# The weights' low parts are written by VectorE alone, in place and in longer pieces

## The reference

```python
for i in range(DEPTH):                      # DEPTH = 2
    u = rms_norm(h, norm_mix[i])
    mix = diff_attention(...) if i % 2 == 0 else moba_attention(...)
    h = h + mix
    u = rms_norm(h, norm_ffn[i])
    ffn = swiglu(u, gate, up, down) if i % 2 == 0 else moe_swiglu(u, router, gate, up, down)
    h = h + ffn
return rms_norm(h, final_norm)
```

## Time and profile before

| | us |
|---|---|
| median of 3 runs | 1608.91 |
| lowest and highest | 1608.26 to 1609.38 |
| span of the profiled execution | 1611.9 |
| TensorE busy in it | 1530.4 (95%) |
| VectorE busy | 1308.2 (81%) |
| ScalarE busy | 1145.0 (71%) |
| GpSimd busy | 619.0 (38%) |

### The profile page before, as it was taken

How to read it: one execution, slowest core, us unless ns; L and a number is a source line. 1 busy time by engine, 2 the same in 40 slices (tenths; PEclk the granted TensorE clock), 3 DMA queues, 4 the chain that set the end, 5 groups by cost and what they waited for, 6 DMA issues and landing times.

```text
span 1611.9 us, 25603 instructions
## 1 busy us (share of the span) xinstructions
PE 1530.4 (95%) x7688; PEld 1240.8 (77%) x7688; DVE 1308.2 (81%) x1820; ACT 1145.0 (71%) x2077; POOL 619.0 (38%) x458
## 2 busy tenths in 40 slices
PE   8998999999996999999999999999999999999997
PEld 7867999988875777777777777777777777777775
DVE  4555444443336999999999999999999999999998
ACT  5555544455543888788788878878888887887886
POOL 2112222221112454444444444445444444454543
PEclk9989999999997999999999999999999999999999
DMA  9723543554311899899899989989989998998970
GB/s 360 261 89 105 199 168 131 207 185 159 130 67 52 295 338 343 290 348 334 305 332 335 334 303 348 328 299 339 339 311 321 338 332 306 345 336 298 331 256 39
DMA packets 178356, 424.48 MB, mean 263 GB/s; under 512 B 4577, under 2 KB 6786, under 8 KB 178306
## 3 DMA queue, kind: packets, MB, share of 16 engines
q1 hardware_dynamic: 178018, 422.77, 73.4%
q10 hardware_dynamic: 288, 1.05, 0.2%
HBM read 422.76 MB, written 1.05 MB: 263 GB/s over the span
## 4 chain that ended last, share of the span: by engine, by line
PE 68%; DVE 13%; issue 11%; ACT 7%; DVEq 1%; POOL 1%; DMA 0%; ACTq 0%; POOLq 0%; SPq 0%
PE psA L1069 9%; PE psA L1070 9%; PE psA L1071 9%; DVE wlo L961 8%; PE psY L1069 6%; PE psY L1071 5%; PE psY L1070 5%; ACT whi L589 5%; PE psB L1069 5%; PE psB L1071 5%; PE psB L1070 5%; PE psY L1165 2%; PE psB L1301 2%; PE psY L1199 1%; PE psY L1088 1%
## 5 line engine op out<-in xcount | busy, mean ns | idle before, releaser
L961 DVE TENSOR_TENSOR wlo<-ring,whi 128x512 fp32r<-128x512 f32 x1012 | 940.2, 984 | 22.6 <-ACT whi L589 17.0
L589 ACT CAST whi<-ring 128x512 fp32r<-128x512 f32 x1349 | 810.2, 623 | 160.5 <-PE psY L1071 54.4
L714 POOL TENSOR_TENSOR wlo<-ring,whi 128x512 fp32r<-128x512 f32 x336 | 510.0, 1518 | 576.4 <-ACT whi L589 572.5
L735 DVE TENSOR_TENSOR wlo<-ring,whi 128x512 fp32r<-128x512 f32 x195 | 140.5, 734 | 194.3 <-ACT whi L434 194.0
L434 ACT CAST whi<-ring 128x512 fp32r<-128x512 f32 x260 | 157.5, 621 | 116.0 <-PE psB L1071 49.8
L672 POOL TENSOR_TENSOR wlo<-ring,whi 128x512 fp32r<-128x512 f32 x65 | 84.4, 1299 | 373.3 <-ACT whi L434 373.3
L1069 PE MATMUL psY<-whi,hhi 128*128 128x512 f32 x496 | 204.5, 412 | 20.4 <-DVE wlo L961 19.6
L1069 PE MATMUL psA<-whi,ihi 128*128 128x512 f32 x448 | 184.6, 412 | 15.7 <-DVE ilo L967 11.4
L1071 PE MATMUL psY<-whi,hlo 128*128 128x512 f32 x496 | 195.8, 395 | 0.0
L1070 PE MATMUL psY<-wlo,hhi 128*128 128x512 f32 x496 | 195.7, 395 | 0.0
L1069 PE MATMUL psB<-whi,ihi 128*128 128x512 f32 x448 | 180.9, 404 | 0.0
(11 more groups left out here) (229 smaller groups left out, 2293.2 us busy)
## 6 DMA issues: line engine op xcount, KB each, us to landing
ring<-in_moe_w_gate SPq DMA_DIRECT2D x56, 2048.0 KB, 7.7
ring<-in_moe_w_up SPq DMA_DIRECT2D x56, 2048.0 KB, 7.7
ring<-in_moe_w_down SPq DMA_DIRECT2D x56, 2048.0 KB, 7.8
ring<-in_moba_w_qkv SPq DMA_DIRECT2D x6, 2048.0 KB, 8.0
ring<-in_diff_w_qkv SPq DMA_DIRECT2D x5, 2048.0 KB, 16.6
ring<-in_ffn_w_gate SPq DMA_DIRECT2D x5, 2048.0 KB, 8.1
ring<-in_ffn_w_up SPq DMA_DIRECT2D x5, 2048.0 KB, 8.9
ring<-in_ffn_w_down SPq DMA_DIRECT2D x5, 2048.0 KB, 7.4
```

The costliest lines, as they stand in the source:

```text
L589: nc.scalar.copy(whi[:, (NG + m) % HL, :], ring[:, r, g * GROUP:(g + 1) * GROUP]).then_inc(hi_done, 1)
L714: nc.gpsimd.tensor_tensor(wlo[:, (NG + m) % HL, :], ring[:, (NS + j) % RING, g * GROUP:(g + 1) * GROUP], f(whi[:, (NG + m) % HL, :]), ALU. ...
L735: nc.vector.tensor_tensor(wlo[:, m % HL, :], ring_group(s, g), f(whi[:, m % HL, :]), ALU.subtract).then_inc(lo_dve, 1)
L961: nc.vector.tensor_tensor(wlo[:, (NG + m) % HL, :], ring[:, (NS + m // GS) % RING, g * GROUP:(g + 1) * GROUP], f(whi[:, (NG + m) % HL, :]) ...
```

## The change

- GpSimd makes no low parts any more. Its loop over items is gone. VectorE makes all of them.
- The low part has no tile of its own. `wlo` is now seven tiles that lie at the addresses of the seven raw ones: the low part is written over the raw weights.
- So a place of the ring is free only when TensorE has used its last group. SyncE waits for `group_used` instead of `lo_dve` and `lo_pool`.
- The space saved goes to `whi`, which is 12 groups deep instead of 6. `AHEAD` is 8 instead of 5.
- VectorE works in pieces: one group for the first 8 groups of the program, 4 groups (128x2048) in the dense feed-forward and in all items, and 2 groups (128x1024) elsewhere. ScalarE works in pieces of 2 groups (128x1024) behind the first 8 groups. Orders that end inside a piece of VectorE are rounded up to its end.
- Behind the last item the engines prepare the first groups of an item that doesn't come. Before, that load was of 1 KB, now it is a full slot of 2 MB.

The core of the diff:

```diff
-HL = 6
-AHEAD = 5
+HL = 12
+AHEAD = 8
...
+    def hi_piece(m):
+        return 1 if m < single else 2
+
+    def lo_piece(m):
+        return 1 if m < single else 4 if m in ffn_groups else 2
...
-        ring = sb("ring", [P, RING, SLOT])
+        raw = ExitStack()
+        ring = [sb(f"ring{r}", [P, SLOT], F32, raw) for r in range(RING)]
+        raw.close()
+        wlo = [sb(f"wlo{r}", [P, SLOT], F32R) for r in range(RING)]
         whi = sb("whi", [P, HL, GROUP], F32R)
-        wlo = sb("wlo", [P, HL, GROUP], F32R)
...
             def load(r, dst, src):
-                sp.wait_ge(lo_dve, dve_past)
-                sp.wait_ge(lo_pool, pool_past)
+                sp.wait_ge(group_used, used_past)
                 sp.dma_start(dst, src).then_inc(slot_full[r], 16)
...
             def item_split(i, first, last):
-                for m in range(first, last):
+                for m in range(first, last, 2):
                     j, g = m // GS, m % GS
-                    r = (NS + j) % RING
                     if g == 0:
-                        act.wait_ge(slot_full[r], slot_landed(i, j))
-                    act.wait_ge(group_used, used_at(i, m - HL + 1))
-                    nc.scalar.copy(whi[:, (NG + m) % HL, :], ring[:, r, g * GROUP:(g + 1) * GROUP]).then_inc(hi_done, 1)
+                        act.wait_ge(slot_full[(NS + j) % RING], slot_landed(i, j))
+                    act.wait_ge(group_used, used_at(i, m + 2 - HL))
+                    nc.scalar.copy(hi_of(NG + m, 2), part_of(ring, NS + j, g, 2)).then_inc(hi_done, 2)
...
-            with pool.Fori(0, n) as i:
-                for m in range(POOL_EVERY - 1, IG, POOL_EVERY):
-                    j, g = m // GS, m % GS
-                    pool.wait_ge(hi_done, used_at(i, m + 1))
-                    nc.gpsimd.tensor_tensor(wlo[:, (NG + m) % HL, :], ring[:, (NS + j) % RING, g * GROUP:(g + 1) * GROUP],
-                                            f(whi[:, (NG + m) % HL, :]), ALU.subtract).then_inc(lo_pool, 1)
...
             def item_halve(i, first, last):
-                for m in range(first, last):
-                    if m % POOL_EVERY != POOL_EVERY - 1:
-                        dve.wait_ge(hi_done, used_at(i, m + 1))
-                        g = m % GS
-                        nc.vector.tensor_tensor(
-                            wlo[:, (NG + m) % HL, :], ring[:, (NS + m // GS) % RING, g * GROUP:(g + 1) * GROUP],
-                            f(whi[:, (NG + m) % HL, :]), ALU.subtract).then_inc(lo_dve, 1)
+                for m in range(first, last, 4):
+                    j, g = m // GS, m % GS
+                    dve.wait_ge(hi_done, used_at(i, m + 4))
+                    nc.vector.tensor_tensor(part_of(wlo, NS + j, g, 4), part_of(ring, NS + j, g, 4),
+                                            f(hi_of(NG + m, 4)), ALU.subtract).then_inc(lo_done, 4)
...
-                    wait_item_group(pe, i, m)
+                    if m % 4 == 0:
+                        pe.wait_ge(lo_done, used_at(i, m + 4))
```

More of the change, by code:

```diff
@@ L124, in trunk @@
     assert IS % RING == 0 and IG % HL == 0 and all(g == GS for _, g in slots[-RING:])
+    assert NG % 4 == 0 and all(g % 4 == 0 for _, g in slots)
     with ExitStack() as ctx:
@@ L315, in f, with part_of, hi_of, wlo_of @@
             return ap.bitcast(F32)
[L317 to L324, removed]
+        def part_of(t, s, g, size=1):
+            return t[s % RING][:, g * GROUP:(g + size) * GROUP]
+        def hi_of(m, size=1):
+            return whi[:, m % HL:m % HL + size, :].rearrange("p g n -> p (g n)")
+        def wlo_of(n):
+            return part_of(wlo, *group_of[n])
         def n_items(eng):
@@ L425, in split_to @@
             def split_to(n):
-                for m in range(split[0], min(n, NG)):
+                n = min(-(-n // lo_piece(n)) * lo_piece(n), NG)
+                while split[0] < n:
+                    m, size = split[0], hi_piece(split[0])
                     s, g = group_of[m]
@@ L730, in halve_to @@
             def halve_to(n):
-                for m in range(halved[0], min(n, NG)):
-                    if not by_pool[m]:
-                        s, g = group_of[m]
-                        dve.wait_ge(hi_done, m + 1)
-                        nc.vector.tensor_tensor(wlo[:, m % HL, :], ring_group(s, g), f(whi[:, m % HL, :]),
-                                                ALU.subtract).then_inc(lo_dve, 1)
-                halved[0] = max(halved[0], min(n, NG))
+                n = min(-(-n // lo_piece(n)) * lo_piece(n), NG)
+                while halved[0] < n:
+                    m, size = halved[0], lo_piece(halved[0])
+                    s, g = group_of[m]
+                    dve.wait_ge(hi_done, m + size)
+                    nc.vector.tensor_tensor(part_of(wlo, s, g, size), part_of(ring, s, g, size), f(hi_of(m, size)),
+                                            ALU.subtract).then_inc(lo_done, size)
+                    halved[0] += size
             def norm_diag(norm):
@@ L1131, in rows_group @@
                     xs = slice(tb * P, (tb + 1) * P)
-                    ins = three(outs[tb][:, half, :], xh[:, xs], xl[:, xs], whi[:, n % HL, :],
-                                wlo[:, n % HL, :], first and k == 0, last and g >= slots[s][1] - 2)
+                    ins = three(outs[tb][:, half, :], xh[:, xs], xl[:, xs], hi_of(n), wlo_of(n), first and k == 0, last and g >= slots[s][1] - 2)
                 ins.then_inc(group_used, 1)
@@ L1322, in item_slot_products @@
                         k, half = divmod(g, 2)
[L1323 removed]
+                        ins = three(psY[:, half, :], hhi[:, k, place_of(c)], hlo[:, k, place_of(c)], wh, wl,
                                     c == 0 and k == 0, c == NE - 1 and k == FBW - 1)
@@ L1326, in item_slot_products @@
                         ps = (psA if kind == "gate" else psB)[:, 0, :]
-                        ins = three(ps, ihi[:, g, :], ilo[:, g, :], whi[:, at, :], wlo[:, at, :], g == 0, g == KD - 1)
+                        ins = three(ps, ihi[:, g, :], ilo[:, g, :], wh, wl, g == 0, g == KD - 1)
                     ins.then_inc(group_used, 1)
```

72 lines of the change are left out of this document (19 added, 53 removed).

## The result

| | us |
|---|---|
| predicted | 1552 (1540 to 1575) |
| kernel after, median of 4 runs | 1581.17 (1579.67 to 1583.4) |
| kernel before on the same chip, median of 4 runs | 1608.59 (1608.15 to 1609.38) |
| ratio | 0.9823, 95% interval 0.9806 to 0.9839 |
| span of the profiled execution after | 1579.0, in a run of 1580.75 |

What follows compares the result with a forecast made beforehand. VectorE was taken to bound the expert loop, TensorE close second. Eight items each 7.2 us shorter and the first expert 1.0 us later gave -56.6 us, from 1608.9 to 1552 us, range 1540 to 1575.

Steps and rivals of the forecast that it cites:

- What bounded the kernel: Expert loop: VectorE sets the pace, busy 131.88 of 135.00 us an item, its pieces slowed by GpSimd; TensorE close second.
- the rival that they would stay at 990: Low parts stay at 990 ns without GpSimd because something else slows them: 1961 us; chance 1%.
- VectorE and ScalarE: Expert loop: low-part pieces of 2.32 us, roundings of 1.043 us; VectorE's item falls to 110.4 us, ScalarE's to 96.
- The item without waits, 127.3 us: Expert loop: one item takes 127.3 us instead of 135.0 if TensorE never waits for low parts.
- Item's start ... loss 0.2 instead of 1.5: Start of each expert item: `ilo` no longer queues behind `wlo` pieces, so TensorE loses 0.2 us instead of 1.5.
- The prediction's own sign of being wrong: Forecast is wrong if an item stays above 130 us; `wlo`, `slot_full` or the DMA as releaser would tell why.
- Coarse pieces behind a gate slot, 0.3: After gate slots in each item: 0.09 us of slack six times, 0.05 us lost each, 0.3 in all.
- Rival 1: Pieces too coarse: TensorE waits 0.5 us at six or seven places an item, 28 us back, 1580 us; chance 13%.
- First expert + 1.0: Start of the expert loop: two pieces of 2.32 us ahead of the first `ilo` delay it 1.0 us, once.
- Dense part 0 within 4: Dense part before the expert loop: no change, with 4 us either way for attention and the deeper `whi`.
- Slots freed by use, bandwidth: Loads in the expert loop: later freeing costs nothing with 25 us of room; 345 GB/s needed, 389 seen.
- Rivals 2 and 3: Loads become the bound, 1571 to 1609 us, chance 5%; loads go one at a time, 1825 us, chance 2%.

Runs made afterwards that it cites:

- experiment 1: Kernel before with all low parts on VectorE in single pieces of 512, separate `wlo` kept, none on GpSimd: 1594.84 us, ratio 0.9906.
- experiment 5: Kernel after with 64 copies, and VectorE's low parts in the expert loop in pieces of 1024 instead of 2048: 1554.6 us, ratio 0.9655.
- 64 copies: Kernel after plus 64 one-column copies into an unread tile on ScalarE in the dense feed-forward, shifting its expert loop: 1564.16 us, ratio 0.973.

## Why the prediction was wrong, step by step

**What bounded the kernel: right.** Without GpSimd the pieces of 512 take 676 to 694 ns (experiment 1); the rival that they would stay at 990 is out.

**VectorE and ScalarE: right.** 2.29 us a piece against 2.32, 1.053 a rounding against 1.043, VectorE 109.3 us an item against 110.4, ScalarE 93.6 against 96.

**The item without waits, 127.3 us: right**, measured 127.32 (experiment 5).

**"Item's start ... loss 0.2 instead of 1.5": the step that failed.** It took ScalarE to be ready when the gather is. The change made ScalarE's program ahead of and in the loop shorter, which moved the loop's body from 715 to 683 and so across the edge of a block. The branch then takes 4.7 us instead of 0.3, `ihi` and `ilo` are late, and TensorE waits 2.2 us, with 1.5 us more in two items for the clock that fell. In all 17 us (1581.2 against 1564.2 with 64 copies), 16 more than counted. It was no rival of mine, and the profile of the kernel before can't show it: its branch takes 0.3 us, with room for 4 instructions and not for 12. The prediction's own sign of being wrong, an item above 130 us, came true, but with neither of the releasers it named for that case: it was `ilo` behind the branch, not `wlo` or a load. The queue q14 and the distance of its packets were there to be asked.

**Coarse pieces behind a gate slot, 0.3: mis-sized**, 1.1 us an item by experiment 5, 6 us more than counted in eight. Rival 1 named this mechanism, but not the places: each is small (0.1 us), and the one of 0.3 is behind the one-hots.

**First expert + 1.0: right.** From the 2900th matmul to the loop's first one the kernel after loses 0.9 us on the kernel before.

**Dense part 0 within 4: off.** The loop's first product with `wlo` comes at 514.6 to 519.0 us in six executions with single groups there (mean 516.3), at 519.0 to 524.2 in nine with pairs in the `wo` slots (mean 521.9): 5.6 us, of which 1.0 was counted as the first expert. That makes some 4.6 us, against 0. What the prediction named for this part (pieces of 1.23 us between the steps of the softmax) is shown for some 2 us of TensorE's waits. But single groups brought the median down by 1.2 to 1.7 us only and the loop's start not at all, so the pieces explain at most a part of the 4.6 us. The clock moves this place by as much as 4 us from one execution to another, and it was at 1.2 GHz for longer in the executions with pairs; whether longer waits bring that about is open.

**Slots freed by use, bandwidth: right.** Loads land in 7.7 to 7.8 us, no engine waits for one in the loop, and 346 GB/s were moved in an item of 127.3. Rivals 2 and 3 are out.

16 + 6 + 5 = 27 of the 29 us between 1552 and 1581; the first two are differences of measured kernels, the last is one of means of profiled executions, and its cause is open. With the stall avoided and pieces of 1024 the kernel takes 1553.4 to 1555, what was forecast for the change, and this is the version to use: 3.5% faster than before.

## What to carry to other kernels

When an edit changes how many instructions stand in or ahead of a loop, look on each engine at how long its branch back takes: "issue" in front of the body's first instruction and more packets on the instruction queue were a fetch in every kernel here, and a few instructions more or less ahead of the loop, or a body of fewer blocks, decided it. Long pieces save an engine time, but before choosing the longest one ask what is queued behind it: half the size cost VectorE 2.8 us an item, which it had to spare, and gave back the 1.1 us that TensorE had not.

## What was not expected of the hardware

- ScalarE and VectorE fetched a loop's body again at each turn once it touched four blocks of 8 KB, at 3 to 6 us a turn; none of the 19 bodies that were run is an exception. In the kernel before, 371 instructions from 715 on cost nothing and the same 371 from 727 on cost 40 us a run.
- Work in a loop's shadow isn't free of place: 64 useless copies made the kernel 17 us faster.
- The granted clock between 110 and 120 us was 0.50 in three executions, 0.63 to 0.66 in five and 0.86 to 0.97 in nine, of kernels with the same or nearly the same code there. Two with the same code, at 0.50 and 0.86, reached their 800th matmul 4.2 us apart.
